# Both MLP projections of a decoder layer as seven block products instead of eight

## The reference, cut to what matters

```
mixed = concat([attn_o, rg], -1) @ w_out          # 2048 x 2048
x = x + mixed
u = rmsnorm(x, norm2_g) @ w_up                    # 2048 x 8192
x = x + jnp.square(jax.nn.relu(u)) @ w_down       # 8192 x 2048
return rmsnorm(x, final_norm_g)
```

## Time and profile before

| | |
|---|---|
| median of 3 runs | 2520.7 us (2519.09 to 2523.78) |
| profiled execution | 2519.1 us, its span from first to last instruction also 2519.1 us |
| PE busy | 2479.0 us, 98% of the span |
| DVE / ACT / POOL busy | 979.7 / 571.9 / 961.7 us |
| DMA | 95 GB/s over the span |
| granted TensorE clock, mean | 0.992 of full speed |

### The profile page before, as it was taken

The page is one execution under the profiler, slowest core; times in us unless marked ns, Lnnn a source line. Parts: engine busy times, 40 slices in busy tenths (PEclk is TensorE's granted clock), DMA queues, the critical chain, the costliest instruction groups (busy, mean ns, idle before and its releaser), DMA issues.

```text
span 2519.1 us, 49369 instructions
## 1 busy us (share of the span) xinstructions
PE 2479.0 (98%) x19880; PEld 2413.6 (96%) x19880; DVE 979.7 (39%) x1522; ACT 571.9 (23%) x712; POOL 961.7 (38%) x402
## 2 busy tenths in 40 slices
PE   8999999999999999999999999999999999999997
PEld 7969899999999999999999999999999999999997
DVE  4268625555555633631331321321321421321465
ACT  5241222222222311311111111111111111111122
POOL 3413323333333544444444444444444444444441
PEclk9999989999999999999999999999999999999998
DMA  6424233333333433333333333333333333333332
GB/s 217 129 63 110 68 82 89 89 94 90 88 88 89 149 91 89 91 92 91 89 90 89 90 91 92 92 92 92 92 92 91 89 89 90 91 91 92 92 87 91
DMA packets 442912, 239.54 MB, mean 95 GB/s; under 512 B 15650, under 2 KB 439778, under 8 KB 441954
## 3 DMA queue, kind: packets, MB, share of 16 engines
q1 hardware_dynamic: 430802, 224.36, 31.4%
q10 hardware_dynamic: 12064, 14.53, 1.6%
HBM read 224.95 MB, written 13.90 MB: 95 GB/s over the span
## 4 chain that ended last, share of the span: by engine, by line
PE 95%; DVE 2%; issue 1%; ACT 1%; DMA 1%; SPq 0%; ACTq 0%; DVEq 0%
PE product L399 88%; PE banks L433 6%; PE banks L430 1%; DMA x_in<-in_x_prompt_dram 1%; DVE a_lo L1257 0%; PE product L433 0%; DVE a_lo L1248 0%; DVE score L1065 0%; ACT relu_p L742 0%; DVE rk L933 0%; ACT a_hi L742 0%; DVE score_s L1112 0%; DVE qam L1121 0%; DVE a_lo L957 0%; ACT out_t L742 0%
## 5 line engine op out<-in xcount | busy, mean ns | idle before, releaser
L367 POOL TENSOR_TENSOR w_lo<-w_raw,w_hi 128x1024 fp32r<-128x1024 f32 x390 | 950.5, 2438 | 1517.8 <-ACT w_hi L739 1517.8
L399 PE MATMUL product<-a_hi,w_hi 128*128 128x260 f32 x4192 | 852.8, 285 | 7.4 <-DVE a_lo L957 3.2
L399 PE MATMUL product<-a_hi,w_lo 128*128 128x260 f32 x4192 | 846.4, 284 | 0.0
L399 PE MATMUL product<-a_lo,w_hi 128*128 128x260 f32 x4192 | 845.0, 283 | 0.0
L739 ACT CAST w_hi<-w_raw 128x1024 fp32r<-128x1024 f32 x390 | 408.2, 1047 | 1794.4 <-PE product L399 1634.4
L399 PEld LDWEIGHTS product<-a_hi,w_hi 128*128 128x128 f32 x4192 | 647.8, 189 | 15.1 <-issue 8.0
L399 PEld LDWEIGHTS product<-a_hi,w_lo 128*128 128x128 f32 x4192 | 647.4, 189 | 0.0
L399 PEld LDWEIGHTS product<-a_lo,w_hi 128*128 128x128 f32 x4192 | 646.0, 189 | 0.0
L399 PE MATMUL product<-b_hi,w_hi 128*128 128x260 f32 x2048 | 414.1, 283 | 0.0
L399 PE MATMUL product<-b_hi,w_lo 128*128 128x260 f32 x2048 | 412.7, 283 | 0.0
L399 PE MATMUL product<-b_lo,w_hi 128*128 128x260 f32 x2048 | 411.8, 283 | 0.0
(11 more groups left out here) (248 smaller groups left out, 1163.9 us busy)
## 6 DMA issues: line engine op xcount, KB each, us to landing
w_raw<-in_w_up_dram SPq DMA_DIRECT2D x128, 512.0 KB, 4.1
w_raw<-in_w_down_dram SPq DMA_DIRECT2D x128, 512.0 KB, 3.8
w_raw<-in_w_in_dram SPq DMA_DIRECT2D x100, 512.0 KB, 3.9
w_raw<-in_w_out_dram SPq DMA_DIRECT2D x32, 512.0 KB, 3.9
x_transposed<-xr ACTq DMA_DIRECT2D x2, 2080.0 KB, 8.0
xr<-x_transposed ACTq DMA_DIRECT2D x1, 4160.0 KB, 13.1
x_in<-in_x_prompt_dram SPq DMA_DIRECT2D x4, 1024.0 KB, 10.3
rs<-in_state_ret_dram SPq DMA_DIRECT2D x8, 512.0 KB, 4.2
```

Of the source, the lines that this page charges most:

```text
L367: nc.gpsimd.tensor_tensor(w_lo[:, slot, :, 0:cols], w_raw[:, raw, :, 0:cols], w_hi[:, slot, :, 0:cols].bitcast(F32), ALU.subtract).then_in ...
L399: last_mm = nc.tensor.matmul(out[:, half, :], w[:, slot, k, 0:cols], a[:, k0 + k, half * HT:(half + 1) * HT], start=(first and k == 0 and ...
```

## The change

The inner dimension, the output features and the tokens of each MLP product are cut in two, and the 2 x 2 block product is done as seven products of half size (the Winograd form of Strassen's algorithm) instead of eight. Rows of the weights alternate between the two inner blocks in steps of 128.

One group now makes two output tiles (up) or four (down): 32 up groups, then 8 chunks x 4 = 32 down groups. A group has seven slots; a slot is one 1024 x 128 weight unit (or 512 x 256) against ONE token half: 24 matmuls. Four slots use loaded weight blocks (slots 0, 2, 3 and 6; the last has block 21 overwritten by a sum) and three use sums of blocks (1, 4, 5; held in PSUM banks 6 and 7, in SBUF in the last three groups). DVE makes the sums, and the low parts of those three; POOL makes the low parts of the other four; ACT all seven high parts. There are six raw buffers in place of two.

The token side has seven combinations too. For up they are made once, around the last output tiles. For down they are made per up group from the squared hidden tiles (`hidden_sums`, `hidden_high`, `hidden_low`), stored to DRAM (`hidden_blocks`, two stores of 910 KB a group) and loaded again by segments (`load_hidden`, 1,040 KB each, seven a chunk) in the down groups. The normed input takes the place of the residual `xr` in SBUF; the residual is stored (`keep_x`) and loaded back after the up part (`load_x`). The up part is finished before the down part begins. The loops over chunks are written out.

The core of the diff, engine by engine (a `window` is one group's stretch of an engine's program). SP:

```
+                n = 4 * g + ("22", "21", "11", "12").index(which) - BLOCKS
+                if n >= 0:
+                    pg, was = n // 4, n % 4
+                    sp.wait_ge(s_lo, lo_pool(pg, (0, 6, 2, 3)[was]))
+                    sp.wait_ge(s_sum, summed(pg, (S_W5, S_W7, S_W6, S_W3)[was]))
...
+            for g in range(GROUPS):
+                if g + 1 < GROUPS:
+                    load_block(g + 1, "11")
+                if g + 2 < GROUPS:
+                    load_block(g + 2, "22")
+                if g == UP_GROUPS - 1:
+                    for s in (1, 2, 3):
+                        load_hidden(0, s)
+                if g == UP_GROUPS:
+                    sp.wait_ge(s_used, done(SLOTS * UP_GROUPS - 1))
+                    for q in range(4):
+                        load_x(q)
+                if g + 2 < GROUPS:
+                    load_block(g + 2, "21")
+                if 1 <= g <= UP_GROUPS:
+                    sp.wait_ge(s_hcl, g)
+                    for part, x in ((0, hc_hi), (1, hc_lo)):
+                        sp.dma_start(hid_dram[g - 1, :, :, part, :], x[:, :, :].bitcast(F32)).then_inc(s_hid, 16)
+                if g == UP_GROUPS - 1:
+                    for s in (0, 4, 5, 6):
+                        load_hidden(0, s)
+                if g + 1 < GROUPS:
+                    load_block(g + 1, "12")
```

POOL, and what PE waits for ahead of slots 3, 4 and 6 of an up group (a down group waits for the same takings, made by DVE):

```
+            for g in range(GROUPS):
+                low_slot(g, 3, "12")
...
+                low_slot(g, 6, "21")
+                if g + 1 < GROUPS:
+                    low_slot(g + 1, 0, "22")
+                    low_slot(g + 1, 2, "11")
...
+                    elif s == 3:
+                        pe.wait_ge(s_ta, taken_act(g, "Y"))
+                    elif s == 4:
+                        pe.wait_ge(s_ta, taken_act(g, "A1"))
+                    elif s == 6:
+                        pe.wait_ge(s_ta, taken_act(g, "A2"))
```

ACT, `window(g)`; the three copies out of the PSUM tensor `Z` are the takings Y, A1 and A2:

```
+                high_slot(g, 3, "12")
...
+                if prev_up:
+                    rectified_squared(g - 1)
+                high_slot(g, 4)
...
+                    act_fn(hb[g % 2][:, 2:4, :], Z[:, x:x + 2, 0:HT], ACT.Identity, scale=-1.0).then_inc(s_ta, 1)
...
+                if prev_up:
+                    hidden_high(g - 1)
...
+                    nc.scalar.copy(hb[g % 2][:, 0, :], Z[:, g % 2, 0:HT]).then_inc(s_ta, 1)
...
+                high_slot(g, 5)
...
+                high_slot(g, 6, "21")
...
+                    high_slot(g + 1, 0, "22")
...
+                    nc.scalar.copy(hb[g % 2][:, 1, :], Z[:, g % 2, 0:HT]).then_inc(s_ta, 1)
...
+                    high_slot(g + 1, 1)
+                    high_slot(g + 1, 2, "11")
```

DVE, `window(g)`:

```
+                if g:
+                    take_a3(g - 1)
...
+                if prev_up:
+                    rectified(g - 1)
...
+                add_block(g, S_W6, "11")
...
+                low_sum(g, S_W6)
...
+                if not is_up(g):
+                    take_y(g)
+                if prev_up:
+                    hidden_sums(g - 1)
+                add_block(g, S_W3, "12")
+                if not is_up(g):
+                    take_a(g, 0)
+                low_sum(g, S_W3)
...
+                if prev_up:
+                    hidden_low(g - 1)
+                if g + 1 < GROUPS:
+                    sum5_7(g + 1)
+                if not is_up(g):
+                    take_a(g, 1)
+                if g + 1 < GROUPS:
+                    low_sum(g + 1, S_W5)
+                take_xy(g)
```

The operands of these DVE operations, in the order `sum5_7` (two of 1024 columns), `add_block` (1024), `low_sum` (1024), `rectified` (1040), `hidden_sums` (the first of four of 260) and `hidden_low` (1820):

```
+                v.tensor_tensor(weight_sum(g), flat(raw[:, b21, :, :]), flat(raw[:, b22, :, :]), ALU.add
...
+                v.tensor_tensor(flat(raw[:, b21, :, :]), flat(raw[:, b21, :, :]), flat(raw[:, b11, :, :]), ALU.add
...
+                v.tensor_tensor(x, x, flat(raw[:, b, :, :]), ALU.add).then_inc(s_sum, 1)
...
+                v.tensor_tensor(flat(w_lo[:, ring(n), :, :]), weight_sum(g), flat(w_hi[:, ring(n), :, :].bitcast(F32)),
...
+                v.scalar_tensor_tensor(out=x, in0=x, scalar=0.0, in1=rb[:, :].unsqueeze(1).to_broadcast([P, 2, T]),
...
+                v.tensor_tensor(h[:, 4, :], h[:, 3, :], h[:, 1, :], ALU.subtract)
...
+                v.tensor_tensor(hc_lo[:, :, :], hb[g % 2][:, :, :], hc_hi[:, :, :].bitcast(F32), ALU.subtract
```

More of the change, by code:

```diff
@@ L29 @@
 CH = 8
-NCHUNK = DFF // (CH * P)
 THIRDS = (0, 32, 64)
@@ L669, in _ @@
                      ready=mixed_split).then_inc(s_used, 1)
[L670 to L673, removed]
+            for t in range(2, KT):
+                m = TILE_OUT + t
+                tile(m, m, unit_of(m), unit_of(m))
             def spread_squares():
@@ L678, in spread_squares @@
                 for half in range(2):
-                    last = mm(B[:, half, 0:HT], ones[:, :], ssum[:, half * HT:(half + 1) * HT])
+                    last = mm(Z[:, 2 + half, 0:HT], ones[:, :], ssum[:, half * HT:(half + 1) * HT])
                 last.then_inc(s_n2m, 1)
[L682 to L694, removed]
+            def product(g, s, out, moving_hi, moving_lo, per, start, ready=None, half=0, of=1):
+                slot = ring(SLOTS * g + s)
+                for k in range(per):
+                    if ready:
+                        ready(k)
+                    at_ = of * k + half
+                    for part, (w, a) in enumerate(((w_hi, moving_hi), (w_hi, moving_lo), (w_lo, moving_hi))):
+                        last = mm(out, w[:, slot, at_, :], a(k), start=(start and k == 0 and part == 0),
+                                  stop=(k == per - 1 and part == 2))
+                return last
@@ new lines, in _ @@
+            for j in range(8):
+                if j < 7:
+                    for u in range(4):
+                        high(unit_of(TILE_OUT) + 4 + 4 * j + u)
+                if j < 7:
+                    h2_pair(j)
+                    if j:
+                        h2_kept(j - 1)
+            high_slot(0, 0, "22")
+            high_slot(0, 1)
+            high_slot(0, 2, "11")
+            h2_pair(7)
+            h2_kept(6)
+            blocks = xr[:, :, :].rearrange("p (k two) n -> p two k n", two=2)
@@ L913, in _ @@
+            for g in range(GROUPS):
+                window(g)
+            squared(KT - 2)
+            for f in range(KT - 4, KT):
                 if f == KT - 1:
@@ new lines, in _, with t2_of_pairs @@
+            add_out(KT - 2)
+            add_square(KT - 2)
+            low_sum(0, S_W5)
+            add_out(KT - 1)
+            sums_of_pair(7)
+            t3_of_pair(6)
+            blocks, lows = (x[:, :, :].rearrange("p (k two) n -> p two k n", two=2) for x in (xr, x_lo))
+            def t2_of_pairs(first, last):
+                dve.wait_ge(s_t3, last)
+                dve.wait_ge(s_used, SLOT0)
+                v.scalar_tensor_tensor(out=t2_sum[:, first:last, :], in0=blocks[:, 0, first:last, 0:HT], scalar=-1.0,
+                                       in1=blocks[:, 0, first:last, HT:T], op0=ALU.mult, op1=ALU.subtract
+                                       ).then_inc(s_t2s, 1)
```

703 lines of the change are left out of this document (539 added, 164 removed).

## The result

Over four executions each, the changed kernel takes 2570.6 us (2566.97 to 2571.94) and the kernel before 2520.8 (2519.09 to 2523.78): the ratio is 1.0195, 95% interval 1.0183 to 1.0208, so it is slower, by 2%. The profiled execution's span is 2570.1 us, 51.0 over the 2519.1 of before. The forecast was 2565.

A forecast was written before the change was run, and what follows sets the result against it. PE's gapless matmuls bound the kernel; fewer help only if other engines keep their cover. 1,536 fewer, -184.5 us, plus 136, 36, 22, 23, 12 and 1 gave +45.5 on 2519.1: 2565 us, range 2420 to 2640.

The forecast's parts named there:

- 31 up windows: Steady up part: each window lasts 24.6 us, 4.4 more than PE's pace, +136 us in all.
- DVE and POOL exclude each other whole, and take turns: DVE operations with two SBUF inputs and POOL operations never overlap; in up windows slot 6's low part holds `hidden_low` until 24.6.
- Block 12 behind the stores: Up windows: the next group's block 12, queued on SP behind two stores, lands 9.5 us after `hidden_low` (8.6 to 10.3).
- PE waits for A1 and for Y: Up windows: PE waits for these two takings, four times under 2 us.
- The clock at its full level: Whole kernel: granted clock assumed at its full level throughout, 1.00 or 2.4 GHz.
- A2 behind two held sums: Down windows: A2 taken at 18.55, PE starts slot 6 1.3 us late; 28 plain windows, +36 us.
- The start: From the last output matmul: group 0 ends at 37.9, not 20.2, and the norm factor adds 6.5; +22 us (12 to 35).
- The passage: Up to down: late block 12, hidden segment and residual make group 32 last 44 us, not 21.5; +23 us (12 to 30).
- The end: Last three windows some 27 us each, +12 (4 to 25); two more DVE operations after the last product, +1.
- holds cost nothing: Rival, chance 0.18: no cost from holds in steady windows, up windows 22.35, down at PE's pace, 2445 us.
- POOL first: Rival, chance 0.16: POOL goes first where both wait, `hidden_low` waits out two operations, up windows 27, 2639 us.
- Full cover: Rival, chance 0.14: neither holds nor block 12 matter, because it lands early; 2366 us.

The follow-up runs named there:

- kernel 3: Changed kernel with block 12 loaded ahead of the two hidden stores and POOL's low parts of loaded slots cut to one eighth: 2373.5 us, ratio 0.9416.
- Kernels 2: Changed kernel with POOL making only one of eight 128-column blocks of each loaded slot's low part, the rest left out: 2467.1 us, ratio 0.9779.
- Kernel 8: Changed kernel with POOL's low part of a loaded slot made by four instructions of 256 columns, not one of 1024: 2463.8 us, ratio 0.9778.
- kernel 5: Changed kernel with DVE taking A2 between the next group's two weight sums in down windows, not behind both: 2539.8 us, ratio 1.0079.
- kernels 1 and 7: 1: changed kernel, block 12 ahead of the stores, 2492.7 us; 7: also `hidden_low` first, A2 between sums, two passage transfers forward, 2438.8 us.
- kernel 9: Changed kernel with POOL's low parts in four pieces, `hidden_low` ahead of slot 5's low sum, A2 between the weight sums: 2388.1 us, ratio 0.9474.

## Why the prediction was right

| step | predicted us | measured us |
|---|---|---|
| matmuls removed | -184.5 | -184.5 (taken over: 64 groups of 20.18) |
| 31 up windows | +136 (24.6 each) | +155 (25.19 each, 5.01 over PE's 20.18) |
| 28 down windows | +36 (1.3 each) | +23 (0.83 each) |
| start | +22 | +16.5 |
| up to down | +23 (group 32: 44) | +24.0 (group 32: 44.2) |
| last three windows | +12 (27 each) | +13.1 (27.2 each) |
| after the last product | +1 | +3.9 (22.2 against 18.3) |
| sum | +45.5 | +51.0, of 51.0 |

The first term is no measurement of its own: at the 20.13 us a group that kernel 3 reaches it would be some -188, and the delays would be counted from that pace. The measured start ends with group 0 and window 1's norm factor, the others are read from intervals of takings. Two of the other six terms are within 1.1 us; two that were too low and two that were too high, by 22 and 19 us, nearly cancel. That the forecast came within 6 us is in part luck: the mechanism is borne out, the sizes only to some 20 us.

- *DVE and POOL exclude each other whole, and take turns*: right, place by place. The point that decides, POOL's slot 6 ahead of `hidden_low` by 0.1 to 0.2 us, was 0.22 in the window shown, and all 32 `hidden_low` were held. `hidden_low` with its hold was put at 4.2 and took 4.10, the first weight sum 3.5 and 3.42, `rectified` 1.8 and 1.94; the second sum was put at its bare 1.25 and took 1.22. Kernels 2 and 8 show the cause. A rule of the Trainium skill (SBUF — State Buffer, section SBUF: two separate sides) says that DVE with two SBUF inputs and GpSimd share one pair of ports as a lock held for a whole instruction. Kernel 8 agrees: four short instructions in place of a long one cut the mean hold of `hidden_low` from 2.04 to 0.38 us.
- *Block 12 behind the stores*: right in kind, and mis-sized. It lands 10.3 and 11.6 us after `hidden_low`'s end in the two windows shown, not 9.5; the upper bound was 10.3. Left out of the walk was SP's own time, 1.35 us from `hidden_low`'s end to the load's issue. From the landing to the end of `hidden_low` the walk was 0.9 too long, 15.1 for 14.2 (10.10 from the landings at 1412.60 and 1438.43 to the start of `hidden_low` in both windows, and 4.10). Together these make the window 25.2 and not 24.6, which is most of the term's error. The rule of the Trainium skill that the prediction weighed (DMA: Bandwidth & Descriptors, section Queues, rings and completion order) is agreed to by this trace: in each of 30 windows the load lands 1.0 to 1.9 us after the second store, though it is much the smaller.
- *PE waits for A1 and for Y*: wrong, without effect on the time. Between 1100 and 1820 us it waits for POOL's low part of slot 3, made from block 12, in 75.5 us of its time (28 times), and for A1 in 9.3. With a load that is later than walked, slot 3 comes last. PE's share in up windows, put at some 82%, reads 87%, because a matmul at the lower clock counts as longer; 1002 matmuls of 120.1 ns are 80% of 150 us.
- *The clock at its full level*: wrong, and without effect. See the last section.
- *A2 behind two held sums*: right; the size was 0.83 and not 1.3, and kernel 5 gives back all of it.
- *The start*: 5.5 us too much. From the last output matmul to the end of group 0 it takes 37.1 us, where 37.9 was put; but the norm factor lengthens window 1 by 2.5 us (27.7 against 25.2) and not by 6.5. Block 12 has no stores ahead of it on SP before group 2, so in window 1 the norm factor takes the place of the late load and does not come on top of it.
- *The passage*: right, but for a slip in the sum: 44 us is 23.8 over the 20.2 that the sum needs, and 21.5 was taken off. Block 12 was put 20.7 us after `hidden_low` and landed 20.9 after (1830.70 to 1851.63). But it was not the only thing late, as kernels 1 and 7 show.
- *The end*: 2.9 us too little was put. From the last taking to the first scaling of the output it takes 8.7 us (2547.95 to 2556.66) where it was 4.3 (2500.80 to 2505.09): among other things PE turns three finished tiles in that time, where it was one. The prediction counted two DVE operations and not these.

Of the rivals, "holds cost nothing" and "POOL first" both fall with `hidden_low`'s 4.10: it waits out one POOL operation, neither none nor two. "Full cover" was put at 2366, and kernel 3, which makes it true by leaving out most of POOL's work, takes 2373.5. So most of the 184.5 us are there to be had, and kernel 9 has 132 of them with the whole computation; the changed kernel spent 197 on two delays that lie in the order of instructions and in the length of POOL's.

## What to carry to other kernels

When an engine off the critical path is given more to do, list its operations with two SBUF inputs, and its copies within SBUF (see the next section), against POOL's operations in time, and price each overlap at a whole POOL instruction; shorter POOL instructions, or a place where POOL is idle, take the price away. On a queue, look at what stands behind a wait, and work it out again after each edit: putting a load ahead of two stores gave 78 us in one version and cost 21 in another, because it was now the load that waited. Two delays in one loop hide each other, so an edit that takes one away shows less than its part, and one that makes something earlier can create a hold that wasn't there.

## What the runs showed of the hardware that was not expected

The granted clock fell within up windows of the changed kernel. Stretches of 2 us (columns as above):

```profile
1440.00:1442.00 2.00, 0.00 (x0) 0.00 (x0) 0.47 (x1) 1.93 (x3) 1.98 (x1) 1.00 0.20 58
1442.00:1444.00 2.00, 1.93 (x12) 1.96 (x13) 1.93 (x5) 0.00 (x0) 0.00 (x0) 0.70 0.00 0
1444.00:1446.00 2.00, 2.00 (x11) 2.00 (x11) 1.50 (x2) 1.61 (x1) 0.00 (x0) 0.50 0.00 0
1446.00:1448.00 2.00, 2.00 (x17) 2.00 (x17) 0.61 (x1) 2.00 (x4) 0.00 (x0) 0.94 0.40 113
```

PE had stood still through 1440 to 1442 and for most of the 2 us before; the clock then went to 0.50 (1.2 GHz) and came back to 1.00 (2.4 GHz). In the window before, where PE did only 0.11 us between 1414 and 1416, it stayed at 1.00, and so it did in kernel 2 between 1250 and 1400 us, where PE is idle for 12% of the time in waits of 2.0 us at most. The dip cost nothing here: from the landing of block 12 to the next `hidden_low` both windows take 10.10 us, with the dip and without, since PE is not in the loop that sets the pace.

Not only operations with two SBUF inputs are held. In the kernel before, DVE's cast of `u` to `b_hi` (L1298) has one input in SBUF and its output there:

```profile
1044.12 0.43 DVE L1298 CAST b_hi<-u 128x520 f32 x1
1052.60 2.40 DVE L1298 CAST b_hi<-u 128x520 f32 x1
...
1052.15 2.56 POOL L367 TENSOR_TENSOR w_lo<-w_raw,w_hi 128x1024 fp32r<-128x1024 f32 x1 [3.30 <-ACT w_hi L739]
```

By itself it takes 0.43 us; begun during a POOL operation it ends 0.29 us after POOL's. So it goes in 62 of its 64 times (2.38 to 2.40 us). DVE makes no such cast in the steady windows of the change, so the prediction is untouched.

Splitting POOL's operation costs it little by itself: in kernel 8 four pieces in a row that DVE did not disturb took 2.85 us (from 1408.78) where one piece takes 2.39.
